# Gated retention and pooling encoder: the four sums of activation quarters move from VectorE to GpSimd

## The reference, cut to what matters

```python
h2 = (_rmsnorm(x, g_ffn) * (1.0 + scale2) + shift2).astype(dt)
up = jnp.einsum('bsd,df->bsf', h2, w_up)          # 1024 -> 2 x 2816
up = _dwconv_centred(up, conv_w, conv_b)          # three taps along the tokens
act, lin = jnp.split(up, 2, axis=-1)
ffn = jnp.einsum('bsf,fd->bsd', jax.nn.gelu(act) * lin, w_down)
return x + gate2 * ffn
```

## Time and profile before

| | |
|---|---|
| median of 3 runs | 2872.68 us (2869.72 to 2874.84) |
| the profiled execution | 2868.03 us, its span 2866.2 us |
| PE busy | 2757.7 us (96%) |
| DVE busy | 1751.2 us (61%) |
| POOL busy | 1112.5 us (39%) |
| ACT busy | 827.3 us (29%) |
| mean granted TensorE clock | 0.983 |

### The profile page before, as it was taken

The page is one execution under the profiler, slowest core; times in us unless marked ns, Lnnn a source line. Parts: engine busy times, 40 slices in busy tenths (PEclk is TensorE's granted clock), DMA queues, the critical chain, the costliest instruction groups (busy, mean ns, idle before and its releaser), DMA issues.

```text
span 2866.2 us, 31884 instructions
## 1 busy us (share of the span) xinstructions
PE 2757.7 (96%) x12703; PEld 2245.3 (78%) x12703; DVE 1751.2 (61%) x2202; ACT 827.3 (29%) x1083; POOL 1112.5 (39%) x704
## 2 busy tenths in 40 slices
PE   5999999999899999999989999999998999999998
PEld 2788888888678888888768888888876888888876
DVE  4362735545786777766776545362758776677766
ACT  4111111111543333333361111111135333333332
POOL 0212222221356666566422221222223665666662
PEclk8999999999999999999999999999999999999999
DMA  9301111110111111111131110201110211111211
GB/s 389 99 30 54 45 42 47 32 53 23 59 30 59 45 59 59 45 52 52 67 128 50 37 49 20 68 30 54 37 52 15 67 52 45 59 44 52 67 37 74
DMA packets 204756, 170.56 MB, mean 60 GB/s; under 512 B 8369, under 2 KB 181697, under 8 KB 201537
## 3 DMA queue, kind: packets, MB, share of 16 engines
q1 hardware_dynamic: 199713, 150.69, 16.7%
q10 hardware_dynamic: 4896, 17.83, 1.6%
HBM read 160.10 MB, written 8.39 MB: 59 GB/s over the span
## 4 chain that ended last, share of the span: by engine, by line
PE 60%; DVE 16%; POOL 11%; ACT 8%; issue 3%; DMA 1%; SPq 0%; ACTq 0%; DVEq 0%; POOLq 0%
PE ps L585 25%; PE ps L928 12%; PE ps L774 12%; POOL f_w L1452 6%; DVE cv L1668 5%; DVE cv L1675 5%; ACT cv L1188 3%; ACT f_w L1133 2%; POOL f_raw L1469 2%; PE ps L781 1%; PE ps L619 1%; PE ps L593 1%; PE ps L957 1%; PE ps L973 1%; PE ps L944 1%
## 5 line engine op out<-in xcount | busy, mean ns | idle before, releaser
L1452 POOL TENSOR_TENSOR f_w<-f_raw,f_w 128x512 fp32r<-128x512 f32 x378 | 549.9, 1468 | 562.7 <-ACT f_w L1133 562.0
L619 PE MATMUL ps<-hc_hi,f_w 128*128 128x512 f32 x2240 | 698.6, 393 | 23.5 <-DVE cv L1668 12.6
L1428 POOL TENSOR_TENSOR w_split<-w_raw,w_split 128x1024 fp32r<-128x1024 f32 x104 | 254.0, 2446 | 981.5 <-ACT w_split L1055 981.5
L619 PEld LDWEIGHTS ps<-hc_hi,f_w 128*128 128x128 f32 x2240 | 423.1, 190 | 117.3 <-DVE u_sb L1651 16.3
L585 PE MATMUL ps<-h_hi,w_split 128*128 128x512 f32 x1792 | 488.9, 391 | 0.0
L774 PE MATMUL ps<-a_split,f_w 128*128 128x512 f32 x1920 | 447.7, 392 | 7.0 <-DVE xT L1704 7.0
L619 PE MATMUL ps<-hc_lo,f_w 128*128 128x512 f32 x1120 | 439.0, 392 | 0.0
L774 PEld LDWEIGHTS ps<-a_split,f_w 128*128 128x128 f32 x1920 | 357.6, 188 | 93.9 <-DVE xT L1704 20.2
L585 PEld LDWEIGHTS ps<-h_hi,w_split 128*128 128x128 f32 x1792 | 334.0, 188 | 68.7
L1133 ACT ACTIVATE f_w<-f_raw 128x512 fp32r<-128x512 f32 x378 | 227.4, 623 | 475.1 <-PE ps L774 235.6
L928 PE MATMUL ps<-w_split,h_hi 128*128 128x512 f32 x1024 | 317.6, 391 | 6.0 <-DVE h_lo L1569 5.6
(11 more groups left out here) (196 smaller groups left out, 3331.6 us busy)
## 6 DMA issues: line engine op xcount, KB each, us to landing
f_raw<-in_w_up SPq DMA_DIRECT2D x176, 256.0 KB, 3.2
w_raw<-in_w_in SPq DMA_DIRECT2D x56, 512.0 KB, 3.8
ada<-in_w_ada SPq DMA_DIRECT2D x24, 1024.0 KB, 8.4
f_raw<-in_w_down SPq DMA_DIRECT2D x88, 256.0 KB, 3.1
xin<-in_x ACTq DMA_DIRECT2D x16, 512.0 KB, 6.2
w_raw<-in_w_in SPq DMA_DIRECT2D x64, 128.0 KB, 2.6
w_raw<-in_w_in SPq DMA_DIRECT2D x32, 256.0 KB, 3.1
w_raw<-in_w_out SPq DMA_DIRECT2D x16, 512.0 KB, 3.2
```

Source lines behind the costliest of these rows:

```text
L619: ins = pe.matmul(ps_row[:, half_of(PRODUCT_BANK[i])], a[:, cols], b, start=k == 0 and n == 0, stop=k == KQ - 1 and n == 2)
L1428: pool.tensor_tensor(w_lo[:, ws, :], w_raw[:, i % 2, :], w_hi[:, ws, :].bitcast(F32), ALU.subtract).then_inc(lo_done.sem, 1)
L1452: pool.tensor_tensor(piece_slot(q)[:, 1, :], piece_raw(q), piece_slot(q)[:, 0, :].bitcast(F32), ALU.subtract).then_inc(piece_lo.sem, 1)
```

## The change

The four sums are issued by POOL, between weight pieces 7 and 8 of its queue, and no more by DVE. POOL waits there for the last modulated piece (`mid_full`) and for the last low part of the plain quarters (`b_lo`), and for its own sums 1 and 3. ACT waits for sum 3 before `a_high(0)`, and DVE for sum 4 before `t_low(6)`.

```diff
@@ act
                 piece_high(where, 9)
+                act.wait_ge(*t_sum.at(mid, 3))
                 a_high(where, 0)
@@ pool
+            def t_sums(dst, a, b):
+                pool.tensor_tensor(dst, a, b, ALU.subtract).then_inc(t_sum.sem, 1)
@@
-                for q in range(6, len(PIECES)):
+                piece_low(where, 6)
+                piece_low(where, 7)
+                full_of = [h_full[seq][:, n, :, :] for n in range(4)]
+                pool.wait_ge(*mid_full.at(mid, 4 * KQ))
+                pool.wait_ge(*b_lo.at(mid, 4 * KQ))
+                t_sums(t_mid[:, :, :], full_of[1], full_of[0])
+                pool.wait_ge(*t_sum.at(mid, 1))
+                t_sums(full_of[1], full_of[3], full_of[1])
+                t_sums(full_of[3], full_of[3], t_mid[:, :, :])
+                pool.wait_ge(*t_sum.at(mid, 3))
+                t_sums(full_of[2], full_of[2], full_of[3])
+                for q in range(8, len(PIECES)):
                     piece_low(where, q)
@@ dve
-            def t_sums(dst, a, b):
-                dve.tensor_tensor(dst, a, b, ALU.subtract).then_inc(t_sum.sem, 1)
@@
-                dve.wait_ge(*mid_full.at(mid, 4 * KQ))
-                t_sums(t_mid[:, :, :], full_of[1], full_of[0])
-                t_sums(full_of[1], full_of[3], full_of[1])
                 t_low(mid, seq, 3, t_mid[:, :, :], 1)
-                t_sums(full_of[3], full_of[3], t_mid[:, :, :])
-                dve.wait_ge(*t_sum.at(mid, 3))
-                t_sums(full_of[2], full_of[2], full_of[3])
@@
                 side_after(where, 1, 0)
+                dve.wait_ge(*t_sum.at(mid, 4))
                 t_low(mid, seq, 6, full_of[3], 3)
```

## The result

The changed kernel took 2877.62 us, the median of 20 runs (2871.76 to 2882.38). The kernel before took 2869.77 us beside it, again over 20 runs (2866.94 to 2874.84). The ratio is 1.0023 with a 95% interval of 1.0016 to 1.0030: slower by 6.6 us, between 4.6 and 8.6 (the two medians themselves differ by 7.85). The forecast was 2879.9 us, the range 2874.5 to 2884.0.

The account below looks back on a forecast made before the run. The prediction took the DVE-ACT-POOL chain, not PE's stall, to set the time. A shift of 3.6 us in each of two sequences gave 7.2 us, added to 2872.68 for 2879.9 us, range 2874.5 to 2884.0.

Parts of the forecast that it names:

- The bound: From the last `b_low` to the residual update, the DVE-ACT-POOL chain sets the time; PE's 5.63 us stall lies beside it.
- A sum on POOL: One subtraction of 2048 elements on POOL takes 4.6 us, kept between 4.5 and 4.8, against 2.29 on DVE.
- The alternation: Low parts and `gated` on DVE exclude POOL's sums for whole instructions; whichever has waited longer goes first.
- The shift: `gated` ends at 805.7 instead of 802.11, 3.6 us later in each sequence, carried on to PE's wait at 839.7.
- POOL keeps its turn between sums 2 and 3: Rival: `t_low(3)` runs only at 795.9, `gated` ends near 809; some 7 us a sequence, 2886 us; chance 0.08.
- the one without hindrance: Rival: long sums do not hinder DVE, `gated` ends at 803.2; 1.1 us a sequence, 2874.9; chance 0.17 together with absorption.
- absorption: Rival: part of the shift is absorbed on the way to 839.70; chance 0.17 together with the one without hindrance.
- The new waits of PE: In set 2, PE waits 3.5 us at product 0, then again, all inside the old wait, moved.
- cover of 2.6 us for weight piece 10: Piece 10's sum on POOL is ready at about 813, ACT reaches it at 815.6, so it is hidden by 2.6 us.
- The turn at `a_low`: After `gated`, POOL goes first as before, no term; rival that DVE wins: 4.7 us in all, 2877.4, chance 0.17.
- The sum: Whole kernel: 2 x 3.6 = 7.2 us slower, over both sequences.
- The 9.2 us taken off DVE are worth nothing: DVE's 9.2 us of relief gains nothing further, since the chain now waits on POOL for what DVE did then.

Follow-up runs that it names:

- e1: The changed kernel again, no edit; one run 2877.46 us, PE's wait for the residual 3.63 us later than in the kernel before.
- e2: Against the changed kernel, sums 3 and 4 back on DVE, only 1 and 2 on POOL; one run 2881.27 us, PE's residual wait +4.90 us against before.
- e3: Against the changed kernel, sums 1 and 2 back on DVE, only 3 and 4 on POOL; one run 2865.80 us, PE's residual wait -1.27 us against before.
- e4: Changed kernel with `t_low(3)` and `t_low(4)` writing zeros, computation left out; one run 2877.76 us, PE's residual wait +2.26 us against before.
- e6: Against e3, the low part of sum 2 moved on DVE behind set 1's `act`-half side taps; 2864.91 us, ratio 0.9980 to the kernel before.
- e7: Changed kernel with each POOL sum cut into two instructions of 128 x 1024; one run 2878.77 us, PE's residual wait +4.48 us against before.
- e5: Against the kernel before, all sums on DVE, but sums 3 and 4 and sum 2's low part later; 2862.79 and 2863.75 us, ratios 0.9974 and 0.9979.

## Why the prediction was right

- **The bound.** That the DVE-ACT-POOL chain and not PE's stall sets the time held: the shift of `gated` (3.66) reached PE's wait as 3.61, and in the kernels before and after, e1 to e4, e6 and e7 the wait lies 34.1 us behind the end of `a_low`, within 0.05. PE's stall before product 2 went from 2.75 us (e6) to 7.04 (e4) beside this. Its length proves nothing, though, because its end moves with the chain too: weight piece 10 waits on ACT for the same chain, and in all of these kernels but e6 the wait is 25.0 to 25.1 us behind PE's restart as well. In e2 the chain that ended last even runs over PE for 11.17 us from the restart on. That the restart alone does not set the time is seen from PE's idle time at the wait (0.28 to 0.39 us at the last one, in every one of them), and from e6, where the restart came 2.88 earlier and the wait 3.15. So PE lay beside the chain with less than 1 us to spare in the kernels before and after, which the prediction did not say; e5 shows what that means: with 3.6 us off `gated`, PE is next.
- **A sum on POOL** was put at 4.6 from the line through two medians; it is 4.61. The Trainium skill (GPSIMD Engine Reference, § 3.1) has 4497 ns for a `tensor_tensor` add of 2048 float32 elements; this trace does not agree, 2.5% more for the subtraction, and the measurement decides.
- **The alternation** by whole instructions, the one that waits longer first, came turn by turn as written: `t_low(3)` 4.86 (some 4.7 forecast), `gated` 2.94 (2.9), sums 3 and 4 held back by about 2. e4 removed the contenders and both sums fell to what they take alone. The Trainium skill (SBUF — State Buffer, § Who interferes with whom) exempts a DVE instruction with at most one SBUF input, outside the 2-port modes; e4's fills agree, the sums beside them took 4.63 and 4.65 us.
- **The shift**: 3.6 forecast, 3.61 and 3.61 measured. The rival that POOL keeps its turn between sums 2 and 3 is refuted by `t_low(3)` at 790.93 + 4.86; the one without hindrance by 6.67 and 6.49; absorption by the unchanged 3.6 at the next waits (at the next one 122.12 after the last `b_low`, before 118.45).
- **The new waits of PE.** Product 0 waited 5.11 us where 3.5 were forecast, without effect: PE had come to it 1.6 us sooner after the last `b_low` than in the profile before, since the first 14 matmuls behind its last wait in the opening took 3.32 us in place of 4.90. The cover of 2.6 us for weight piece 10 held: POOL had its sum ready at 815.18, ACT began on it at 817.76.
- **The turn at `a_low`** fell to POOL again, 809.01 against 809.10. So this chance of 0.17 did not come in, and e7 shows it was a real one: 0.04 us decided it there. In both executions of the changed kernel it was POOL's, in both sequences, for the reason given: the situation is that of before.
- **The sum** of 7.2 us stands beside 6.6 (4.6 to 8.6) measured. The forecast time was 2.3 us too high for another reason: its base, a median of three runs (2872.68), lay 2.9 over that of twenty, while the medians differ by 0.65 more than the 7.2.
- **What was not seen.** "The 9.2 us taken off DVE are worth nothing" was true of all four together, but it hid two opposite halves: sums 3 and 4 off DVE gain 1.27 us a sequence, sums 1 and 2 lose 4.90. And that sum 4 stands on the chain at 790.88 while its low part comes at 815.75 was in the rows of before; taking it and sum 3 later on DVE gains 3.44 (e5), nearly as much as the change loses.

## What to carry to other kernels

Before work is moved to a slower engine, ask which pieces the chain waits for at once and which are merely in its way: the first lose by the whole difference in speed, the second may need only be issued later on the engine that they are on, as in e5. Where a DVE instruction with two SBUF inputs stands beside a POOL instruction that reads SBUF, cost each meeting as the rest of the other's whole instruction, follow the turns in order, and expect that a shorter or removed contender hands the meeting to the next instruction. Splitting the long instruction helps the one that waits, and can hurt the chain if the split work is what the chain waits for.

## What the runs showed of the hardware that was not expected

- A fill of 128 x 2048 float32 on DVE took 1.76 us beside POOL's subtraction and did not lengthen it (4.63, 4.65, alone 4.61). What the fill takes alone no run shows.
- The one that has waited needs a little less after the other's end than it takes alone: sum 3 4.48 and sum 4 4.42 for 4.61, `t_low` 2.15 for 2.29.
- With the same instructions, the time from the first to the last `b_low` varied from 33.1 to 36.0 us between executions and sequences, as much as the effect studied. Only distances from a mark right ahead of the change told it to 0.1 us.
